# A hybrid decoder block with 32 experts on one Trainium2 core: 96-row scatters, an early block count, a paired final norm, and further blocks in turns of two

## The reference, cut to what matters

```python
h2 = _rmsnorm(x, norm2_g)
logits = h2 @ router_w + router_b
top_vals, top_idx = lax.top_k(logits, 4)
gates = softmax(top_vals)
# for each expert e, over the tokens that chose it:
u = h2[tokens] @ w_up[e] + b_up[e]                # 1024 -> 2048
a = min(u[::2], 7) * sigmoid(1.702 * min(u[::2], 7)) * (clip(u[1::2], -7, 7) + 1)
y = a @ w_down[e] + b_down[e]                     # 1024 -> 1024
x[tokens] += gates * y
return _rmsnorm(x, final_norm_g)
```

## Time and profile before

| what | value |
|---|---|
| median of three runs | 1413.06 us |
| the profiled execution's own time | 1411.97 us |
| its span, first to last instruction | 1410.2 us |
| TensorE busy | 1341.1 us (95%) |
| VectorE, ScalarE, GpSimd busy | 84%, 75%, 19% |
| mean granted TensorE clock | 0.986 of full speed |
| moved by DMA | 459.82 MB, mean 326 GB/s |

### The profile page before, as it was taken

One profiled execution on the slowest core, in us unless ns is written; L12 is line 12 of the kernel. 1 busy time (PEld: TensorE's weight loads), 2 busy tenths in 40 slices (PEclk: granted clock), 3 DMA queues, 4 the chain that ended last, 5 costly groups with the idle time before them and its releaser, 6 DMA issues.

```text
span 1410.2 us, 19064 instructions
## 1 busy us (share of the span) xinstructions
PE 1341.1 (95%) x6393; PEld 1060.0 (75%) x6394; DVE 1185.5 (84%) x1063; ACT 1059.1 (75%) x895; POOL 268.1 (19%) x134
## 2 busy tenths in 40 slices
PE   7999989989999999999999999999999999999991
PEld 6888866558887777777777777777777877778771
DVE  5566645478999999999999999999999999999993
ACT  6454333326788989888898989898988889898962
POOL 0000000000123133221222231322312122213120
PEclk9999999999999999999999999999999999999996
DMA  8422153227899999999999999999999999999954
GB/s 250 133 60 75 46 212 146 90 90 309 315 384 405 408 415 408 415 403 408 399 419 398 415 402 412 405 412 406 410 404 399 409 398 420 397 420 393 422 179 150
DMA packets 71828, 459.82 MB, mean 326 GB/s; under 512 B 7317, under 2 KB 36149, under 8 KB 47152
## 3 DMA queue, kind: packets, MB, share of 16 engines
q1 hardware_dynamic: 64560, 438.12, 76.5%
q0 software_dynamic: 7232, 21.22, 6.4%
HBM read 443.35 MB, written 20.19 MB: 329 GB/s over the span
## 4 chain that ended last, share of the span: by engine, by line
PE 73%; DMA 16%; issue 4%; DVE 4%; ACT 3%; SPq 0%; ACTq 0%; DVEq 0%
PE psum L1788 47%; DMA w_raw_pair<-w_up 14%; PE psum L1554 8%; PE psum L1551 3%; PE psum L1804 3%; PE psum L1781 2%; PE psum L1640 2%; PE psum L1771 1%; PE psum L1682 1%; DMA w_buf<-w_out 1%; PE psum L1664 1%; ACT lin L775 1%; DVE w_low L1217 1%; ACT sig L776 1%; PE psum L1929 1%
## 5 line engine op out<-in xcount | busy, mean ns | idle before, releaser
L1217 DVE TENSOR_TENSOR w_low<-w_raw_pair,w_high 128x2048 fp32r<-128x2048 f32 x384 | 861.4, 2285 | 59.9 <-ACT w_high L742 59.0
L742 ACT ACTIVATE w_high<-w_raw_pair 128x2048 fp32r<-128x2048 f32 x384 | 721.7, 1914 | 116.9 <-PE psum L1788 56.7
L1788 PE MATMUL psum<-w_high,x_high 128*128 128x512 f32 x1024 | 275.9, 391 | 0.0
L1788 PE MATMUL psum<-w_low,x_high 128*128 128x512 f32 x1024 | 273.9, 389 | 0.0
L1788 PEld LDWEIGHTS psum<-w_low,x_high 128*128 128x128 f32 x1024 | 192.2, 188 | 40.3
L1788 PEld LDWEIGHTS psum<-w_high,x_high 128*128 128x128 f32 x1024 | 191.2, 188 | 40.1 <-issue 0.4
L565 POOL DMA_INDIRECT residual_rows<-y_rows,scatter_rows x32 | 148.9, 4653 | 364.1 <-ACT y_rows L781 364.1
L1788 PE MATMUL psum<-w_high,a_high 128*128 128x512 f32 x512 | 161.9, 397 | 0.0
L1788 PE MATMUL psum<-w_low,a_high 128*128 128x512 f32 x512 | 158.2, 390 | 0.0
L1788 PE MATMUL psum<-w_high,x_low 128*128 128x512 f32 x544 | 149.8, 397 | 0.5 <-DVE x_low L1388 0.5
L1788 PEld LDWEIGHTS psum<-w_high,x_low 128*128 128x128 f32 x544 | 99.4, 188 | 26.7 <-issue 5.8
(11 more groups left out here) (290 smaller groups left out, 1474.8 us busy)
## 6 DMA issues: line engine op xcount, KB each, us to landing
w_raw_pair<-w_up SPq DMA_DIRECT2D x128, 2048.0 KB, 14.8
w_raw_pair<-w_down SPq DMA_DIRECT2D x64, 2048.0 KB, 14.6
w_in_raw<-w_in SPq DMA_DIRECT2D x28, 512.0 KB, 3.8
w_buf<-w_out SPq DMA_DIRECT2D x2, 2048.0 KB, 10.9
x_rows<-x SPq DMA_DIRECT2D x4, 512.0 KB, 5.4
x_rows<-x SPq DMA_DIRECT2D x1, 2048.0 KB, 18.5
residual_rows<-x_rows SPq DMA_DIRECT2D x4, 512.0 KB, 2.6
normed_rows<-h_rows SPq DMA_DIRECT2D x4, 512.0 KB, 2.6
```

Of the source, the lines that this page charges most:

```text
L742: act.activation(wh[:, q.slot(m, SPL), :], raw[q.slot(m, RAW)][:, :], ACT.Copy).then_inc(wh_ready, 1)
L1217: dve.tensor_tensor(wl[q.slot(m, RAW)][:, :], raw[q.slot(m, RAW)][:, :], wh[:, q.slot(m, SPL), :].bitcast(F32), ALU.subtract).then_inc(wl_ ...
L1788: ins = pe.matmul(o[:, j, :], x_part, w_part[:, j * 512:(j + 1) * 512], start=(first and n == 0), stop=(last and n == len(passes) - 1))
```

## The change

**Scatters.** Two constants are new, `FULL = 4` and `STEP = P // 4 = 32`. The big experts of ranks 0 to 3 keep scatters of 128 rows; those of rank 4 and more get 96, so an expert there with more than 96 rows would need a further block. POOL's loop of 14 passes is cut in two, 5 with 128 rows and 9 with 96; the scatters of places 29 and 31 behind it also have 96. `small_row` becomes `cut_row` (0, 1 or 2 steps of 32 rows), for which `order_experts` has two operations more.

**Order in a big step.** On ACT and DVE the work that stood at n = 3 stands at n = 2.

**Early count.** The number of further blocks is worked out by `further_blocks` on DVE, between the second and the third expert, and signalled as `blocks_known`. What is left of `overflow_items` stays at the end. `MAXX` is 24; the loops have `TURNS` = 12 passes, with an inner loop of two blocks each, and every engine waits for `items_ready` inside the turn, SP also before it loads the residual.

**The end.** SP loads the gain (into another place) before it waits for `items_ready` and `blocks_added`. ACT issues one root ahead of the norm. Mean, root and refinement are done for two tiles at once.

```diff
-MAXX = 16
+MAXX = 24
+TURNS = MAXX // 2
+FULL = 4
+STEP = P // 4
...
-        GF = over("final_g_rows", [P, D], shared + 16384)
+        GF = over("final_g_rows", [P, D], hg0)
...
@@ SyncE
+            sp.wait_ge(S("blocks_known"), 1)
+            nx = sp.value_load(CNT[0:1, 0:1], min_val=0, max_val=TURNS)
+            with sp.Fori(0, TURNS) as turn:
+                with sp.If(nx > turn):
+                    sp.wait_ge(S("items_ready"), 1)
+                    with sp.Fori(0, 2) as half:
+                        j = turn * 2 + half
+                        ex = sp.value_load(CNT[0:1, bass.ds(j + MAXX, 1)], min_val=0, max_val=NE - 1)
+                        step(over_chunks(j), ex, ex)
+
+            sp.wait_ge(chunk_used, nx * (2 * NC) + LAST.count(UPC - 2))
+            sp.dma_start(GF[:, :], final_g.rearrange("(o d) -> o d", o=1).to_broadcast([P, D])).then_inc(S("gf_in"), 16)
             sp.wait_ge(S("items_ready"), 1)
-            nx = sp.value_load(CNT[0:1, 0:1], min_val=0, max_val=MAXX)
-            with sp.Fori(0, MAXX) as j:
-                with sp.If(nx > j):
-                    ex = sp.value_load(CNT[0:1, bass.ds(j + MAXX, 1)], min_val=0, max_val=NE - 1)
-                    step(over_chunks(j), ex, ex)
-
-            sp.wait_ge(blocks_added, nx + (NE + 1))
-            sp.dma_start(GF[:, :], final_g.rearrange("(o d) -> o d", o=1).to_broadcast([P, D])).then_inc(S("gf_in"), 16)
+            sp.wait_ge(blocks_added, nx * 2 + (NE + 1))
             for i in range(TT):
                 sp.dma_start(XF[:, i, :], accv[:, i, :]).then_inc(S(f"xf_in{i}"), 16)
...
@@ GpSimd
-            with pool.Fori(0, PAIRS) as i:
-                scatter(i * 2 + 1, expert_at(i * 2 + 1))
+
+            def pair(i, rows):
+                scatter(i * 2 + 1, expert_at(i * 2 + 1), rows)
                 gather(i * 2 + 5, expert_at(i * 2 + 5), use_x(i * 2 + 4))
                 scatter(i * 2 + 2, expert_at(i * 2 + 2), PH)
                 gather(i * 2 + 6, expert_at(i * 2 + 6), use_x(i * 2 + 5), PH)
-            scatter(NE - 3, expert_at(NE - 3))
+
+            with pool.Fori(0, FULL + 1) as i:
+                pair(i, P)
+            with pool.Fori(FULL + 1, PAIRS) as i:
+                pair(i, P - STEP)
+            scatter(NE - 3, expert_at(NE - 3), P - STEP)
             scatter(NE - 2, expert_at(NE - 2), PH)
-            scatter(NE - 1, expert_at(NE - 1))
+            scatter(NE - 1, expert_at(NE - 1), P - STEP)
...
@@ ScalarE, big_step (the same edit in VectorE's big_step)
-                    if n == 3:
+                    if n == 2:
                         x_high(use_x(p))
                         silu_half(fold)
                         bias_row(BSU, UPPER, of_place(UPPER, p), bsu_ready)
...
@@ ScalarE, the end
+            act.activation(warm[:, 1:2], warm[:, 0:1], ACT.Sqrt).then_inc(S("tables"), 1)
             for i in range(TT):
                 act.wait_ge(S(f"xf_in{i}"), 16)
                 act.activation(YF[:, i, :], XF[:, i, :], ACT.Square, accum_out=ss1[:, i:i + 1]).then_inc(S("ssf"), 1)
-                act.wait_ge(S("mean_eps"), 5 + TT + i)
-                root(act, r1[:, i:i + 1], ss1[:, i:i + 1])
+                if i % 2:
+                    act.wait_ge(S("mean_eps"), 5 + TT + i // 2)
+                    root(act, r1[:, i - 1:i + 1], ss1[:, i - 1:i + 1])
...
@@ VectorE
+                link(dve.tensor_scalar(cut_steps, rank, float(FULL), cst("free")[0:NE, 0:1], ALU.is_ge, ALU.mult))
+                link(dve.tensor_tensor(cut_steps, cut_steps, is_small, ALU.add))
...
+            def further_blocks():
+
+                ext, cnt = small[:, 96:128], small[:, 160:192]
+                link(dve.scalar_tensor_tensor(cnt, cut_row[:, :], float(STEP), counts, ALU.mult, ALU.add))
                 link(dve.tensor_scalar(ext, cnt, float(P), None, ALU.is_gt))
                 for k in range(2, TT + 1):
                     link(dve.scalar_tensor_tensor(ext, cnt, float(k * P), ext, ALU.is_gt, ALU.add))
                 link(dve.tensor_tensor_scan(last, ones[:, 0:NE], ext, 0.0, ALU.mult, ALU.add))
+                link(dve.tensor_scalar(ext[:, 0:TURNS], cst("item")[:, 0:TURNS], 2.0, last[:, NE - 1:NE], ALU.mult, ALU.is_lt))
+                link(dve.tensor_reduce(cnt[:, 0:1], ext[:, 0:TURNS], AX.X, ALU.add))
+                dve.tensor_copy(CNT[:, 0:1], cnt[:, 0:1]).then_inc(S("blocks_known"), 1)
...
                 split(SECOND, n)
+            further_blocks()
             small_step(2, THIRD)
...
-            for i in range(TT):
-                dve.wait_ge(S("ssf"), i + 1)
-                mean_eps(ss1[:, i:i + 1], ss1[:, i:i + 1], D)
-                link(refined(r1[:, i:i + 1], ss1[:, i:i + 1], rtmp[:, 0:1]))
-                dve.scalar_tensor_tensor(YF[:, i, :], XF[:, i, :], r1[:, i:i + 1], GF[:, :], ALU.mult, ALU.mult
-                                         ).then_inc(S("out_ready"), 1)
+            for n in range(TT // 2):
+                r = slice(2 * n, 2 * n + 2)
+                dve.wait_ge(S("ssf"), 2 * n + 2)
+                mean_eps(ss1[:, r], ss1[:, r], D)
+                link(refined(r1[:, r], ss1[:, r], rtmp[:, 0:2]))
+                for i in range(2 * n, 2 * n + 2):
+                    dve.scalar_tensor_tensor(YF[:, i, :], XF[:, i, :], r1[:, i:i + 1], GF[:, :], ALU.mult, ALU.mult
+                                             ).then_inc(S("out_ready"), 1)
```

More of the change, by code:

```diff
@@ L281, in hybrid_moe_block @@
         rt = small[:, 256:264].rearrange("p (a t) -> p a t", t=TT)
-        itf = small[:, 264:280]
+        itf = small[:, 192:192 + MAXX]
         warm = small[:, 280:284]
-        key_col, rank, is_small, place = (small[0:NE, 112 + n:113 + n] for n in range(4))
+        key_col, rank, is_small, place, cut_steps = (small[0:NE, 112 + n:113 + n] for n in range(5))
         key_row, diag, perm = order_work[:, 0:NE], order_work[:, NE:2 * NE], order_work[:, 2 * NE:3 * NE + 1]
@@ L593, in _ @@
                 gather(i * 2 + 6, expert_at(i * 2 + 6), use_x(i * 2 + 5), PH)
-            scatter(NE - 3, expert_at(NE - 3))
-            scatter(NE - 2, expert_at(NE - 2), PH)
-            scatter(NE - 1, expert_at(NE - 1))
[L597 to L604, removed]
+            with pool.Fori(0, FULL + 1) as i:
[3 more added lines that the diff above has]
+            scatter(NE - 3, expert_at(NE - 3), P - STEP)
+            scatter(NE - 2, expert_at(NE - 2), PH)
+            scatter(NE - 1, expert_at(NE - 1), P - STEP)
+            pool.wait_ge(S("blocks_known"), 1)
+            nx = pool.value_load(CNT[0:1, 0:1], min_val=0, max_val=TURNS)
+            with pool.Fori(0, TURNS) as turn:
+                with pool.If(nx > turn):
+                    with pool.Fori(0, 2) as half:
+                        j = turn * 2 + half
+                        pool.wait_ge(slot_ready, j + 1)
+                        pool.wait_ge(gathered, (j + NE) * 16)
+                        gather(j + NE + 1, 0, None)
+                        scatter(j + NE, 0)
         def root(act, r, mean):
@@ L897, in _ @@
             gated(NE - 1, e31)
[L898 to L913, removed]
+            act.wait_ge(S("blocks_known"), 1)
+            nx = act.value_load(CNT[0:1, 0:1], min_val=0, max_val=TURNS)
+            with act.Fori(0, TURNS) as turn:
+                with act.If(nx > turn):
+                    with act.Fori(0, 2) as half:
+                        j = turn * 2 + half
+                        q = over_chunks(j)
+                        act.wait_ge(S("items_ready"), 1)
+                        ex = act.value_load(CNT[0:1, bass.ds(j + MAXX, 1)], min_val=0, max_val=NE - 1)
+                        bias_row(BSU, UPPER, of_expert(UPPER, ex), bsu_ready)
+                        bias_row(BSD, LOWER, of_expert(LOWER, ex), bsd_ready)
+                        x_high(j * 3 + (OVER + 1))
+                        for n in range(UPC):
+                            cast(q, n, n)
+                        silu(j + NE, q.count(UPC - 1, 1))
+                        a_high(j * 3 + (OVER + 2))
+                        for n in range(UPC, NC):
+                            cast(q, n, n)
+                        gated(j + NE, 0)
+            act.activation(warm[:, 1:2], warm[:, 0:1], ACT.Sqrt).then_inc(S("tables"), 1)
             for i in range(TT):
@@ L1474, in _ @@
             overflow_items()
[L1475 to L1490, removed]
@@ new lines, in _ @@
+            nx = dve.value_load(CNT[0:1, 0:1], min_val=0, max_val=TURNS)
+            with dve.Fori(0, TURNS) as turn:
+                with dve.If(nx > turn):
+                    with dve.Fori(0, 2) as half:
+                        j = turn * 2 + half
+                        ex = dve.value_load(CNT[0:1, bass.ds(j + MAXX, 1)], min_val=0, max_val=NE - 1)
+                        q = over_chunks(j)
+                        dve.wait_ge(blocks_added, j + NE + 1)
+                        make_sel(ex, block_off[:, bass.ds(j, 1)])
+                        slot_rows(j * 3 + OVER, 0)
```

(29 more changed lines are left out.)

56 lines of the change are left out of this document (19 added, 37 removed).

## The result

The changed kernel takes 1402.09 us, the median of five runs (1399.80 to 1406.31), against 1413.06 us: a ratio of 0.9927, with a 95% interval from 0.991 to 0.9944. Timed again beside other kernels it gave 0.9926 (0.9914 to 0.9939). The forecast was 1400.6 us, in a range from 1396 to 1406.

A forecast was written before the change was run, and what follows sets the result against it. The prediction took the DMA as the loop's limit, with TensorE within 2% of it. Scatters 6.1, order 1.6 and tail 4.8 us sum to 12.5 us, from 1413.06 to a median of 1400.6 us, range 1396.0 to 1406.0.

The forecast's parts named there:

- The limit: Expert loop: the DMA sets the pace, so passes from the fifth on shorten to 64.3 to 64.5 us, earlier ones stay 65.2.
- Part 1: Scatters in passes 5 to 13: 32 rows fewer at 21 ns a row, 0.68 us each, 6.1 us in all.
- Rival B: Scatters: a row costs its bytes once, 9.4 ns, so nine cuts give 2.7 us; time 1404.0 us; chance 0.13.
- Part 2: Big steps, n = 3 to n = 2: the bias row's wait goes; 1.6 us gained once, bounds nothing and 11.3 us.
- chunk 8 of the small step: Loop: the next late point after the bias row, where TensorE takes up DVE's split with 1.6 us of slack.
- Part 3: Early count on DVE: costed at nothing because covered; up to 1.9 us without the cover.
- Part 4: Tail: earlier residual request and landing give 3.0 us, the norm 1.8 us; 4.8 us in all.
- the norm: Tail: first tile to end of last scaling, done by pairs with the root's table loaded ahead, 11.96 to 10.15 us.
- The table load: Tail: ACT's root table load, 1.28 us, goes ahead and is done by 1389.5, 2.7 us before the first tile.
- rival D: Tail gives nothing: ACT's table load or the loads' landing takes its place; 1405.4 us; chance 0.09.
- (a) to (c): Tail: SP's loop ends before the landing, 0.7 us; last scatter has 96 rows, 0.6 us; gain's issue goes, 0.40 us.
- The sum: Whole kernel: 6.1 + 1.6 + 4.8 = 12.5 us saved, median 1400.6 us.

The follow-up runs named there:

- e4_plain: The changed kernel with scatters that write instead of add, leaving out the sum over experts: 1393.88 us, ratio 0.9868.
- e2_scatters: The kernel before with only the big scatters of rank 4 and more cut to 96 rows: 1406.91 us, ratio 0.9964.
- e1_order: The kernel before with only the extra work of big steps moved from n = 3 to n = 2: 1411.30 us, ratio 0.9997.
- e6_n3: The changed kernel with the extra work of big steps back at n = 3: 1403.40 us, ratio 0.9935.
- e8_small_n2: The changed kernel with the extra work of small steps also moved from n = 3 to n = 2: 1401.89 us, ratio 0.9921.
- e5_late_count: The changed kernel with further_blocks moved to the end, just ahead of overflow_items: 1402.17 us, ratio 0.9921.
- e3_tail: The changed kernel with 128-row scatters for all big experts and big steps' extra work back at n = 3: 1409.58 us, ratio 0.9978.
- e10_tail_maxx16: The kernel of e3_tail with MAXX = 16 instead of 24: 1408.66 us, ratio 0.9971.
- e7_tight: The changed kernel with scatter rows cut to the counts of these inputs: 1397.73 us, ratio 0.9888.
- e9_tight_small: The changed kernel with the scatter rows of e7_tight and the small steps' order of e8_small_n2: 1394.93 us, ratio 0.988.

## Why the prediction was right, and where it wasn't

**The limit.** Right. The DMA set the pace from pass 3 on; passes 3 and 4 did not get shorter, those from 5 on did, and e4_plain shows the other side, where TensorE is the limit at 64.00 us.

**Part 1, scatters: 6.1 us forecast, 4.3 to 5.4 measured** (the loops of e2_scatters and of the changed kernel). The mechanism held; the term was mis-sized. The forecast took 21 ns a row from one 10 us stretch. The passes give 18 ns, 0.57 us for 32 rows. Rival B's 9.4 ns is what the bytes cost once, and e4_plain shows what it leaves out: the addition, about 11 ns more. The Trainium skill's fit (DMA: Bandwidth & Descriptors, Anatomy of one DMA) gives the same 0.30 us for 32 rows, an estimate; the 0.57 us of the passes decide.

**Part 2, order: 1.6 us forecast, nothing clear of noise measured.** The medians give 0.4 us alone (e1_order) and 1.3 us in the changed kernel (e6_n3). The loops of single profiles run from 0.5 us longer (e1_order) over 0.6 and 1.0 us shorter (the changed kernel against e2_scatters) to 2.5 and 3.0 us shorter (against e6_n3). The step of the reasoning that failed is "That is chunk 8 of the small step". I looked for the next late thing, found one with 1.6 us of slack, and didn't look at the start of the small step, where `x_low_half` stood behind three splits with 0.7 us. The changed kernel and e1_order both wait there. Even 0.7 us did not show as a gain where the waits begin: counted from TensorE's first expert matmul, pass 3 starts 0.3 us later in the changed kernel's first profile than before, and at the same time in the second. And when e8_small_n2 removed that wait as well, the split took over, as the reasoning said it must.

**Part 3, the count: nothing forecast.** e5_late_count agrees within 0.5 us of median. One thing is open. Four of four profiles that contain the tail's edits with n = 3 or a late count (e3_tail 1006.50, e10_tail_maxx16 1005.29, e6_n3 1001.45, e5_late_count 1000.81) have loops 1.3 to 2.6 us longer than the kernel with the same scatters without them (1003.9, or 999.54); the changed kernel (998.94, 998.50) does not. This goes with the tail's part, worth 5.1 and 4.7 us in the tail, giving only 3.1 and 4.1 us in time. In e3_tail and e10_tail_maxx16 half of it or more comes early: pass 2 takes 65.39 and 65.27 us there, and 64.37 and 64.03 in the two profiles of the kernel before, so the weights are late one pass sooner. Neither MAXX nor the place of the count explains it by itself, and no run here tells what does.

**Part 4, the tail: 4.8 us forecast, 5.5 and 4.9 in the profiles.** By its steps, forecast and first profile: from the scatter's issue to the request of the residual 7.32 to 5.6, and 5.63 came; from there to the first square 5.47 to 4.2, and 3.56 came, below the bound of 3.8 that I had taken; the norm 11.96 to 10.15, and 9.84 came. The table load was done 2.4 us ahead of the first square (forecast 2.7), so that rival D had no place. Of the three edits (a) to (c) the profiles give the sum only; e5_late_count shows that the place of the count isn't among the necessary ones.

**The sum.** 12.5 us forecast; 11.0 us between the medians, and 10.3 to 10.4 by the first ratio and by the second timing's ratio and medians. By the two pairs of profiles 2.7 and 2.3 us are missing in the loop: 0.7 to 1.8 us of part 1, the rest of part 2, which one profile each cannot separate better. The last down half's 1.6 us, which no term held, are missing too; the tail gave 0.7 and 0.1 us more than forecast. That the parts alone give 0.4 + 5.1 + 3.1 = 8.6 us and 10.3 together is within their intervals.

## What to carry to other kernels

When two engines lie within 2% of each other, ask of the fuller queue first. Here TensorE's waits that hung on a transfer in a full queue were symptoms, and reordering the work around them moved the wait more than the time. Take bytes off the queue instead, and count them as the queue does: a row that is added in memory cost 18 ns here, where its bytes cost 9.4. Before pricing a stall's removal, list the slack of every hand-over in the period, not of one.

## What the runs showed of the hardware

**Adding against writing.** The last scatter of 96 rows landed 3.7 us after its issue when it wrote, and 5.2 to 5.6 us when it added; adding took 4.8 us for 64 rows and 6.1 for 128, all without other traffic. The landing and the queue's share in the changed kernel, over 25 us, and in e4_plain, over 24 us:

```profile
q0 software_dynamic: 112, 0.39, 11.3%
residual_rows<-y_rows,scatter_rows POOLq DMA_INDIRECT x1, 5.6
```

```profile
q0 software_dynamic: 112, 0.39, 5.5%
residual_rows<-y_rows,scatter_rows POOLq DMA_INDIRECT x1, 3.7
```

As a share of 16 engines that is 45 us of engine time for adding 96 rows and 21 us for writing them, about double.

**The granted clock after a short gap.** Ahead of the last down half TensorE stands idle for 1.92 us, waiting for `a_low`, before and after the change alike. In the changed kernel the granted clock of the next 4 us was 0.57 of full speed, in the kernel before 1.00 (the column before the DMA share):

```profile
1360.00:1364.00 4.00, 3.68 (x9) 2.98 (x10) 3.86 (x6) 0.22 (x1) 1.45 (x1) 0.57 0.27 19
```

```profile
1368.50:1372.50 4.00, 3.98 (x18) 3.29 (x19) 3.69 (x10) 0.00 (x0) 1.46 (x1) 1.00 0.35 37
```

A mean of 0.57 says that most of that stretch ran at the lower of the two levels, 1.2 GHz against 2.4, and it costs 1.6 us. Eight of the fourteen profiles have the last step 1.5 us longer or more, and in just these eight the granted clock of the 4 us after the gap is 0.57 to 0.69; in the other six it is 1.00. e1_order, with nothing but the order changed, is among the eight, and e7_tight and e9_tight_small, which hold the whole change, are among the six. So it isn't due to the change; what decides it, no run here tells.

**The time to the first expert matmul** varied from 324.96 to 328.90 us over the fourteen profiles, without an edit there that goes with it. A single profile's span is thus no measure of a change of 3 us; the cut at common places of the timeline is.
